# MLP 1 of a four-block transformer step: six of eight fc1 groups as block products, fc2 by groups of four fc1 tiles, job tiles issued by SP

## The chip, the core and the metric

The kernel runs on one core of one Trainium2 chip. The metric is device time in microseconds (us) of one execution. Five engines work side by side, each with its own in-order queue: PE (TensorE, matmuls; PEld is its weight load), DVE (VectorE), ACT (ScalarE), POOL (GpSimd) and SP (SyncE, which here only issues DMAs). They wait for each other on semaphores.

## The reference, cut to what matters

The reference runs 512 latent tokens and 256 context tokens of width 1024 through two blocks of a first model (layers l0, l1) and two of a second (s0, s1). The part touched is the MLP of l0, which handles latents and context together, 768 tokens:

```python
def _sq_relu_mlp(h, w1, w2):          # w1: 1024 x 4096, w2: 4096 x 1024
    a = jnp.maximum(h @ w1, 0)
    return (a * a) @ w2

h = x * (1 + sc2) + sh2
x = _layer_norm(DEEPNORM_ALPHA * x + g2 * _sq_relu_mlp(h, w_fc1[l], w_fc2[l]), ln2_g[l], ln2_b[l])
```

Shift, scale and gate come from a modulation product `silu(c) @ w_mod[l] + b_mod[l]` for two conditions. All values are float32.

## The kernel before, in words

Features lie on the 128 partitions, tokens along the free axis. A matmul of full precision is made of three: each operand is split into a high part (rounded, a copy by ACT) and a low part (the rest, a subtraction by DVE), and PE adds high x high, low weight x high, high weight x low. So each weight tile, 128x1024 (512 KB), is loaded by SP (L537), copied by ACT (`act_split`, L590) and subtracted by DVE (`dve_split`, L622). High parts have NS = 3 buffers: the copy of tile a waits until PE is through tile a - 3. A list written once for all engines (`tile_order`) fixes the order of the tiles; every engine walks it with `pe_tiles`, `act_tiles`, `dve_tiles`.

MLP 1 (l0) is `mlp`: four quarters, each eight fc1 tiles and then eight fc2 tiles. A tile is 8 steps of k with 3 matmuls over 512 and 3 over 256 tokens (L866, L870). fc1 results go to PSUM in turn to two double banks, ACT takes the ReLU (L1252), DVE squares (L1276), ACT makes the high part (L1254), DVE the low part (L1279). fc2 results are added, gated, into the residual by DVE (`dve_add_gated`, L924).

MLP 2 and 4 (l1, s1; 512 tokens) are `eighths`: eight groups of four fc1 tiles. The first group is plain; the other seven form the 4 tiles as a 2x2 block product after Strassen with seven products instead of eight (`product`, L1378, 24 matmuls of 256 columns each). The sums of weight blocks are made by DVE (`dve_block_sum`, L600), the sums of results too (`sum_of`, L1546), the sums of the token operand once (`operand`, L1524; `operand_high`, `operand_low`). fc2 is done per group: eight outputs of four k steps (`outputs`, L1399, L1404), each added to the residual by DVE (`update`, L1592). Results go to four single banks there. MLP 3 (s0) is `quarters`.

Beside MLP 1 and MLP 3 runs `modulation`: beside MLP 1 132 jobs (128 with a 512 KB tile, 4 that spread a condition). A job is one multiply-and-reduce on DVE (L731) over a tile in a ring of NM = 3 buffers. The jobs are spread over steps 2 to 61 of the MLP's 64 tiles; ACT issues the load of job n + 3 after job n (`act_send`, L691). Weight tiles have NR = 4 landing buffers; XR = 4 more come from the end of l1's attention on.

## Time and profile before

| | us |
|---|---|
| median of 3 runs (lowest, highest) | 2992.75 (2991.43, 2995.24) |
| profiled execution | 2994.86 |
| its span on the core | 2993.5 |
| PE busy | 2843.4 (95%) |
| DVE busy | 1878.0 (63%) |
| ACT busy | 1197.9 (40%) |
| granted TensorE clock, mean | 0.98 |

The profiled execution lies 2.1 us above the median and within the spread of the runs; 1.4 us of it lie outside the span. MLP 1 takes the span from about 515 to 1066 us. Rows of a timeline are start, length, engine, line, operation; several instructions can be merged in one (xN), and a bracket at the end gives the idle time before and what ended it.

### The profile page before, as it was taken

The numbers are of one execution on the slowest core, as the hardware profiler recorded it, in microseconds if no ns is written. First come the engines' busy times: TensorE is split into PE (matmuls) and PEld (weight loads), VectorE is DVE, ScalarE is ACT, GpSimd is POOL, SyncE is SP. The second block draws the span as 40 slices with busy tenths as digits, with TensorE's granted clock in tenths as the row PEclk, the third lists the DMA queues.
The fourth block names the chain that finished last, engine by engine and source line by source line (L and its number), as shares of the span: only waits on it lengthen the run. The fifth ranks groups of instructions, "written<-read, shape, count | busy, mean of one in ns | idle before, by whom it ended". The sixth has DMA issues, their size and how long they took to land. (4 is left out here: it accounts for less than half of the span.)

```text
span 2993.5 us, 43305 instructions
## 1 busy us (share of the span) xinstructions
PE 2843.4 (95%) x17474; PEld 2304.2 (77%) x17474; DVE 1878.0 (63%) x2790; ACT 1197.9 (40%) x1963; POOL 340.7 (11%) x371
## 2 busy tenths in 40 slices
PE   7999999999999989999899999999899999899998
PEld 6766667888888867766688886776567999678896
DVE  3655544656565746664687766546736788567775
ACT  4245543412122242554444545212533444444443
POOL 2022220300000030321301002000420000110000
PEclk9999999999999999999999999999999999999999
DMA  7222001466565511001232332222014555422331
GB/s 282 78 93 85 8 16 49 163 196 210 171 211 189 190 56 51 13 15 57 90 99 78 106 120 64 95 64 64 8 59 159 164 182 168 143 62 87 106 106 64
DMA packets 88495, 315.98 MB, mean 106 GB/s; under 512 B 9991, under 2 KB 12295, under 8 KB 88040
## 3 DMA queue, kind: packets, MB, share of 16 engines
q1 hardware_dynamic: 59040, 213.94, 22.3%
q10 hardware_dynamic: 29256, 99.26, 10.0%
q8 instruction: 140, 2.29, 0.3%
q14 instruction: 59, 0.48, 0.0%
HBM read 311.06 MB, written 2.10 MB: 105 GB/s over the span
## 5 line engine op out<-in xcount | busy, mean ns | idle before, releaser
L866 PE MATMUL bank<-t 128*128 128x512 f32 x4064 | 1011.1, 360 | 24.7 <-DVE t L622 7.7
L866 PEld LDWEIGHTS bank<-t 128*128 128x128 f32 x4064 | 673.1, 190 | 163.1 <-issue 40.5
L590 ACT ACTIVATE t<-t 128x1024 fp32r<-128x1024 f32 x410 | 431.0, 1055 | 759.4 <-PE bank L870 253.9
L622 DVE TENSOR_TENSOR t<-t 128x1024 fp32r<-128x1024 f32 x410 | 508.5, 1244 | 328.3 <-ACT t L590 324.1
L870 PE MATMUL bank<-t 128*128 128x512 f32 x2032 | 606.7, 358 | 4.4 <-POOL t L1181 4.2
L870 PEld LDWEIGHTS bank<-t 128*128 128x128 f32 x2032 | 335.1, 190 | 71.0 <-POOL t L1181 10.3
L1399 PE MATMUL bank<-t 128*128 128x512 f32 x1024 | 308.8, 397 | 1.6 <-ACT t L1469 1.6
L1378 PEld LDWEIGHTS bank<-t 128*128 128x128 f32 x2352 | 283.0, 189 | 4.1 <-ACT t L590 2.3
L1378 PE MATMUL bank<-t 128*128 128x256 f32 x2352 | 283.8, 282 | 2.1 <-ACT t L590 2.1
L1399 PEld LDWEIGHTS bank<-t 128*128 128x128 f32 x1024 | 190.0, 188 | 56.0 <-issue 4.8
L731 DVE SCALAR_TENSOR_TENSOR t<-t 128x1024 f32<-128x1024 f32 x176 | 209.3, 1223 | 2.2 <-DMA t<-in_mod 1.8
L1404 PE MATMUL bank<-t 128*128 128x512 f32 x512 | 187.2, 396 | 0.0
L1898 POOL TENSOR_SCALAR t<-t 128x768 f32<-128x768 f32 (+3 forms) x160 | 125.7, 789 | 522.8 <-DVE t L1866 522.7
L924 DVE SCALAR_TENSOR_TENSOR t<-bank,t 128x512 f32<-128x512 f32 (+1 forms) x128 | 81.6, 664 | 148.5 <-PE bank L870 131.3
L1697 PE MATMUL bank<-t 64*128 64x384 f32 (+2 forms) x768 | 137.0, 475 | 16.5 <-ACT t L1796 5.2
L1841 DVE TENSOR_REDUCE t<-bank 128x1 f32<-128x768 f32 (+1 forms) x120 | 96.6, 846 | 88.3 <-PE bank L1706 68.1
L1786 ACT ACTIVATE t<-bank 128x384 f32<-128x384 f32 (+1 forms) x160 | 73.6, 460 | 172.4 <-PE bank L1714 172.0
L1714 PEld LDWEIGHTS bank<-t 128*128 128x128 f32 x784 | 85.8, 141 | 58.7 <-issue 29.9
L1714 PE MATMUL bank<-t 128*128 128x128 f32 x784 | 121.2, 283 | 10.0 <-DVE t L1852 7.0
L1796 ACT ACTIVATE t<-bank,t 128x768 f32<-128x768 f32 (+3 forms) x160 | 124.1, 780 | 14.1 <-DVE t L1841 8.0
L992 ACT ACTIVATE t<-t 128x512 f32<-128x512 f32 (+1 forms) x64 | 43.8, 684 | 214.7 <-DVE t L924 126.4
L1592 DVE SCALAR_TENSOR_TENSOR t<-bank,t 128x512 f32<-128x512 f32 x128 | 93.7, 747 | 48.1 <-PE bank L1404 47.8
(363 smaller groups left out, 3387.9 us busy)
## 6 DMA issues: line engine op xcount, KB each, us to landing
t<-in_mod ACTq DMA_DIRECT2D x176, 512.0 KB, 4.4
t<-in_l0fc SPq DMA_DIRECT2D x64, 512.0 KB, 4.2
t<-in_l1fc SPq DMA_DIRECT2D x64, 512.0 KB, 3.6
t<-in_s0fc SPq DMA_DIRECT2D x64, 512.0 KB, 3.7
t<-in_s1fc SPq DMA_DIRECT2D x64, 512.0 KB, 3.6
t<-in_mod SPq DMA_DIRECT2D x48, 512.0 KB, 4.4
t<-in_mixin SPq DMA_DIRECT2D x24, 512.0 KB, 3.6
t<-in_l0in SPq DMA_DIRECT2D x12, 512.0 KB, 3.8
```

The costliest lines, as they stand in the source:

```text
L590: act.activation(high_of(key), landed_of(key), ACT.Copy).then_inc(*up("act_whi", a))
L622: dve.tensor_tensor(low_of(key), landed_of(key), high_of(key).bitcast(F32), ALU.subtract).then_inc(*up("dve_wlo", a))
L731: dve.scalar_tensor_tensor(x, x, 1.0, sil[:, :], ALU.mult, ALU.mult, accum_out=modt[L][:, j, s:s + 1]).then_inc(*up("dve_job", (name, n)))
L866: pe.matmul(acc.ap[:, o:o + m], w[:, ws], Hh[:, k, o:o + m], start=k == order[0] and w is hi, stop=False)
L870: ins = pe.matmul(acc.ap[:, o:o + m], hi[:, ws], Hl[:, k, o:o + m], start=False, stop=k == order[-1])
L1378: ins = pe.matmul(dst, w[:, ws], x, start=pair == 0 and k == 0 and w is hi and x is high, stop=pair == 1 and k == 3 and x is low)
L1399: pe.matmul(banks[s].ap, w[:, ws], Ah[:, k, :], start=first and w is hi, stop=False)
L1404: ins = pe.matmul(banks[s].ap, hi[:, ws], Al[:, k, :], start=False, stop=last)
L1697: ins = pe.matmul(places[side][:, 512 * r + o:512 * r + o + m], g["q"][side](c), g["k"][side][:, k0:k0 + m], start=r not in begun, stop=last)
L1714: ins = pe.transpose(turns[r].ap[:, P * b:P * b + P], p[:, P * i:P * i + P], mat("ident"))
L1796: act.activation(keys_of(p, g), scores_of(ps[side], g), ACT.Exp, bias=row[:, 7:8], accum_out=row[:, 3:4]).then_inc(*ps[side].freed((tag, u ...
L1898: pool.tensor_scalar(x, x, stat(u, side)[:, 7:8], 1.0, ALU.mult, ALU.mult).then_inc(*up("pool_prob", (tag, u, side)))
```

## The change

MLP 1 is now `eighths` too, for 768 tokens: groups 0 and 1 plain, groups 2 to 7 as block products of 384 columns (`PLAIN_GROUPS`, `G` in the functions). A product needs two matmul targets of 384 columns, that is a double bank, and of these there are three (`ps0`, `ps1`, `ps2`), against four single ones for 512 tokens. fc2 outputs alternate between two of them. The jobs are spread over steps 2 to 123: a plain group has 24 steps (3 at each fc1 tile, 3 at each fc2 tile), a product group 13 (3, 3, 3, 4 at its four fc2 tiles). Their loads are issued by SP, sorted among the weight tiles by place. The extra four landing buffers come from the end of l0's attention on. `mlp` is gone; names in `quarters` change only.

```diff
@@ memory and order
-                self.slot[key], self.slot_after[key] = NR + a - G, ("l1out", 1)
+                self.slot[key], self.slot_after[key] = NR + a - G, ("l0out", 1)
+PLAIN_GROUPS = {"l0": 2, "l1": 1, "s0": 2, "s1": 1}
@@ mlp_order, for l0, l1, s1
+    for Q in range(8):
+        if Q < PLAIN_GROUPS[name]:
+            for m in range(0 if Q else 2, 4):
+                t.tile((name + "fc1", 4 * Q + m))
+        else:
             t.quad(name + "fc1", Q)
         for j in range(4):
             t.tile((name + "fc2", 4 * Q + j))
@@ sp_tiles
-        for _, _, i, send in sorted(tiles + mods, key=lambda x: x[0:2]):
+        jobs = [(place, place, n, send) for place, n, send in sent_jobs]
+        for _, _, i, send in sorted(tiles + mods + jobs, key=lambda x: x[0:2]):
             send(i)
@@ modulation
-        def act_send(n):
+        def sp_send(n):
             L, condition, s, j = jobs[tiles_[n]]
-            act.dma_start(modw[:, n % NM, :], din[f"mod{L}"][j]).then_inc(*up(f"job_in{n % NM}", (name, n), 16))
+            SPQ.wait_ge(*(at("dve_job", (name, n - NM)) if n >= NM else at("pe_mod", seq.mods[seq.mod_keys[-1]])))
+            sp.dma_start(modw[:, n % NM, :], din[f"mod{L}"][j]).then_inc(*up(f"job_in{n % NM}", (name, n), 16))
@@ eighths
+                *steps, pool_all = modulation(name, sil, jobs, 2, 124, lambda step: eighths_place(name, G, step))
+    PRODUCT_BANKS = {NT: (0, 1, 2, 3, 0, 2, 3), T: (2, 0, 1, 2, 1, 2, 0)}
+    OUT_BANKS = {NT: (1, 0, 2, 3), T: (1, 0)}
+        places = {key: fours[m % 4] if n == NT else ps[m % 4 % 3] for m, key in enumerate(first)}
+    def steps_behind(G, Q, j):
+        if Q < G:
+            return range(24 * Q + 12 + 3 * j, 24 * Q + 15 + 3 * j)
+        o = 24 * G + 13 * (Q - G)
+        return range(o + 3 * j, o + 3 * j + (4 if j == 3 else 3))
+    def eighths_place(name, G, step):
+        for Q in range(8):
+            for j in range(4):
+                if step in steps_behind(G, Q, j):
+                    return seq.place[fc2(name, Q, j)] - 0.5
+                if Q < G and step in steps_beside(G, Q, j):
+                    return seq.place[fc1(name, 4 * Q + j)] + 0.2
@@ act_eighths and dve_eighths, a plain group
                 for m in range(4):
-                    dve_tiles(fc1(name, 0, min(m + 2, 3)))
-                    evict(m)
+                    dve_tiles(fc1(name, 4 * Q + min(m + 2, 3)))
+                    evict(Q, m)
+                    if step:
+                        for s in steps_beside(G, Q, m):
+                            step(s)
@@ dve_eighths, each fc2 tile
-                dve_tiles(fc2_pair(name, Q, j))
+                dve_tiles(fc2(name, Q, j))
...
+                if step:
+                    for s in steps_behind(G, Q, j):
+                        step(s)
                 for m in (2 * j, 2 * j + 1):
                     update(Q, m)
```

**Place 1: DVE at fc2.** On DVE, before, two neighbouring fc2 tiles of MLP 1's first quarter (L622 weight split, L731 job, L924 update of the residual from PSUM, double bank 1 and then 0):

```order
L622 TENSOR_TENSOR t5<-t4,t3 128x1024 [waits s_act_whi,s_tile_in2]
L731 SCALAR_TENSOR_TENSOR t2,t17<-t2,t63 128x1024 [waits s_job_in0]
L731 SCALAR_TENSOR_TENSOR t2,t17<-t2,t63 128x1024 [waits s_job_in1]
L924 SCALAR_TENSOR_TENSOR t1<-bank1,t16,t1 128x512 [waits s_pe_tile,s_pool_x]
L924 SCALAR_TENSOR_TENSOR t1<-bank1,t16,t1 128x256
L622 TENSOR_TENSOR t5<-t4,t3 128x1024 [waits s_act_whi,s_tile_in3]
```

Now, on DVE, the first fc2 tile of group 0 (L612 split, L714 job, L1548 update):

```order
L612 TENSOR_TENSOR t5<-t4,t3 128x1024 [waits s_act_whi,s_tile_in2]
L714 SCALAR_TENSOR_TENSOR t2,t17<-t2,t63 128x1024 [waits s_job_in0]
L714 SCALAR_TENSOR_TENSOR t2,t17<-t2,t63 128x1024 [waits s_job_in1]
L714 SCALAR_TENSOR_TENSOR t2,t17<-t2,t63 128x1024 [waits s_job_in2]
L714 SCALAR_TENSOR_TENSOR t2,t17<-t2,t63 128x1024 [waits s_job_in0]
L1548 SCALAR_TENSOR_TENSOR t1<-bank1,t16,t1 128x512 [waits s_pe_half,s_pool_x]
L1548 SCALAR_TENSOR_TENSOR t1<-bank1,t16,t1 128x256
L1548 SCALAR_TENSOR_TENSOR t1<-bank0,t16,t1 128x512 [waits s_pe_tile,s_pool_x]
L1548 SCALAR_TENSOR_TENSOR t1<-bank0,t16,t1 128x256
```

A tile has two outputs instead of one, and its jobs stand between the split and both of the updates.

**Place 2: ACT at the start of a plain group.** On ACT, before, a tile inside MLP 1's first quarter (L590 split of a weight tile, L1252 ReLU out of a bank, L1254 high part, L691 loads for jobs):

```order
L590 ACTIVATE t3<-t4 128x1024 [waits s_tile_in1]
L1252 ACTIVATE t56<-bank0 128x768 [waits s_pe_tile]
L1254 ACTIVATE t53<-t58 128x768 [waits s_dve_asq]
L691 DMA t2<-in_mod1 128x1024 [waits s_dve_job] x2
L590 ACTIVATE t3<-t4 128x1024 [waits s_tile_in2]
```

Now, on ACT, the start of group 1 (L580 split, L1414 ReLU, L1419 high part):

```order
L580 ACTIVATE t3<-t4 128x1024 [waits s_pe_tile,s_tile_in2]
L580 ACTIVATE t3<-t4 128x1024 [waits s_pe_tile,s_tile_in3]
L580 ACTIVATE t3<-t4 128x1024 [waits s_pe_tile,s_tile_in0]
L1414 ACTIVATE t62<-bank0 128x768 [waits s_dve_alo]
L1419 ACTIVATE t60<-t62 128x768 [waits s_dve_asq]
L580 ACTIVATE t3<-t4 128x1024 [waits s_pe_tile,s_tile_in1]
L1414 ACTIVATE t62<-bank1 128x768 [waits s_dve_alo]
```

Three weight splits stand ahead of the group's first ReLU; the third of them waits for PE to be through the group's second fc1 tile.

**Place 3: DVE from the last product to the first outputs.** On DVE, now, group 2 (L1502 sum of a product out of its bank, L1529 low part, L590 sum of weight blocks); before, MLP 1 has no such place:

```order
L1502 TENSOR_TENSOR t62<-bank0,t62 128x768 [waits s_pe_tile]
L1529 TENSOR_TENSOR t61<-t62,t60 128x2x384 [waits s_act_a,s_act_ahi] x2
L612 TENSOR_TENSOR t52<-t51,t3 128x1024 [waits s_act_whi,s_tile_in7]
L590 TENSOR_TENSOR t4<-t51 128x1024 [waits s_tile_in6,s_tile_in5]
L714 SCALAR_TENSOR_TENSOR t2,t17<-t2,t63 128x1024 [waits s_job_in0,s_b7_read,s_b6_read]
L714 SCALAR_TENSOR_TENSOR t2,t17<-t2,t63 128x1024 [waits s_job_in1]
L714 SCALAR_TENSOR_TENSOR t2,t17<-t2,t63 128x1024 [waits s_job_in2]
L1548 SCALAR_TENSOR_TENSOR t1<-bank1,t16,t1 128x512 [waits s_pe_half]
L1548 SCALAR_TENSOR_TENSOR t1<-bank1,t16,t1 128x256
```

The last product and the second output share bank 0; between the bank's reading and the first update stand two low parts, a split, a block sum and three jobs. At the first fc2 tile of the six product groups stand 3, 3, 4, 4, 3, 3 jobs, and at the last 4, 4, 4, 5, 5, 3.

## Rows read from the trace of the kernel before

**Rows 1.** page, part 1: busy us (share of the span) and instructions of each engine

```profile
PE 2843.4 (95%) x17474; PEld 2304.2 (77%) x17474; DVE 1878.0 (63%) x2790; ACT 1197.9 (40%) x1963; POOL 340.7 (11%) x371
```

**Rows 2.** stretches of MLP 1: length, busy PE, PEld, DVE, ACT, POOL; PEclk, DMA share, GB/s

```profile
536.00:603.00 67.00, 67.00 (x386) 58.55 (x387) 46.51 (x57) 23.45 (x27) 15.03 (x8) 1.00 0.61 202
...
938.00:1005.00 67.00, 67.00 (x385) 58.45 (x384) 45.61 (x60) 19.99 (x22) 0.00 (x0) 1.00 0.61 194
```

**Rows 3.** timeline (start, length, engine, line, operation), PE in MLP 1: two k steps that follow each other

```profile
650.67 0.51 PE L870 MATMUL bank<-t 128*128 128x512 f32 x2
...
651.72 0.51 PE L870 MATMUL bank<-t 128*128 128x512 f32 x2
```

**Rows 4.** timeline, PE in MLP 4 (s1): a group's products, then its fc2

```profile
2722.67 20.16 PE L1378 MATMUL bank<-t 128*128 128x256 f32 x168
2742.72 2.09 PE L1399 MATMUL bank<-t 128*128 128x512 f32 x8
...
2748.42 0.63 PE L1399 MATMUL bank<-t 128*128 128x512 f32 x2
...
2755.43 0.62 PE L1399 MATMUL bank<-t 128*128 128x512 f32 x2
```

**Rows 5.** groups by line and shape, 600 to 1300 us: count | busy us, mean ns | idle before

```profile
L731 DVE SCALAR_TENSOR_TENSOR t<-t 128x1024 f32<-128x1024 f32 x114 | 134.7, 1221 | 1.4 <-DMA t<-in_mod 1.1
...
L622 DVE TENSOR_TENSOR t<-t 128x1024 fp32r<-128x1024 f32 x70 | 86.8, 1242 | 73.1 <-ACT t L590 72.0
...
L924 DVE SCALAR_TENSOR_TENSOR t<-bank,t 128x512 f32<-128x512 f32 x32 | 24.0, 751 | 74.7 <-PE bank L870 72.9 <-ACT t L721 1.6
L1279 DVE TENSOR_TENSOR t<-t 128x768 fp32r<-128x768 f32 x24 | 23.0, 959 | 21.9 <-ACT t L1254 21.9
...
L1254 ACT ACTIVATE t<-t 128x768 fp32r<-128x768 f32 x24 | 20.3, 846 | 26.9 <-DVE t L1276 26.9
...
L924 DVE SCALAR_TENSOR_TENSOR t<-bank,t 128x256 f32<-128x256 f32 x32 | 15.2, 475 | 0.0
```

**Rows 6.** timeline, POOL and DVE at the start of MLP 1

```profile
535.82 5.36 POOL L1185 TENSOR_SCALAR t<-t 128x768 f32<-128x768 f32 x3
...
537.39 1.19 DVE L1276 TENSOR_TENSOR t<-t 128x768 f32<-128x768 f32 x1 [0.47 <-ACT t L1252]
```

**Rows 7.** timeline, start of MLP 2 (l1): operand sums, fc2, third ReLU, PE's wait

```profile
1465.72 5.69 DVE L1524 TENSOR_TENSOR t<-t 128x1024 f32<-128x1024 f32 x4
...
1478.38 2.29 PE L1399 MATMUL bank<-t 128*128 128x512 f32 x8
...
1481.23 0.58 ACT L1464 ACTIVATE t<-bank 128x512 f32<-128x512 f32 x1
...
1483.37 0.96 PE L1399 MATMUL bank<-t 128*128 128x512 f32 x3 [1.25 <-ACT t L1469]
```

**Rows 8.** timeline, MLP 4: from the seventh product's sum to the update

```profile
2743.24 0.68 DVE L1546 TENSOR_TENSOR t<-bank,t 128x512 f32<-128x512 f32 x1
...
2743.96 0.63 ACT L1481 ACTIVATE t<-t 128x512 f32<-128x512 f32 x1 [0.86 <-DVE t L1546]
...
2745.88 0.69 DVE L1573 TENSOR_TENSOR t<-t 128x512 fp32r<-128x512 f32 x1 [1.36 <-ACT t L1484]
2746.83 1.23 DVE L622 TENSOR_TENSOR t<-t 128x1024 fp32r<-128x1024 f32 x1 [0.26 <-ACT t L590]
...
2749.11 1.41 DVE L1592 SCALAR_TENSOR_TENSOR t<-bank,t 128x512 f32<-128x512 f32 x2
```

**Rows 9.** page, part 6: DMA issues, us to landing

```profile
t<-in_mod ACTq DMA_DIRECT2D x176, 512.0 KB, 4.4
```

**Rows 10.** timeline, DVE in MLP 1: two jobs in a row

```profile
640.98 1.22 DVE L731 SCALAR_TENSOR_TENSOR t<-t 128x1024 f32<-128x1024 f32 x1
...
642.12 1.22 DVE L731 SCALAR_TENSOR_TENSOR t<-t 128x1024 f32<-128x1024 f32 x1
```

**Rows 11.** view by stretches, norm and start of MLP 1; columns as in rows 2

```profile
518.00:522.00 4.00, 3.77 (x14) 2.83 (x13) 4.00 (x8) 4.00 (x8) 2.71 (x3) 0.57 0.03 6
```

More of the change, by code:

```diff
@@ L299, in eighths_order @@
             t.tile((name + "fc2", 4 * Q + j))
-    t.mark((name, "end"))
-def mlp_order(t, name):
-    t.tile((name + "fc1", 0))
-    t.tile((name + "fc1", 1), 1)
-    for q in range(4):
-        for m in range(NK):
-            if 8 * q + m > 1:
-                t.tile((name + "fc1", 8 * q + m))
-            t.mark((name, "evict", q, m))
-        for m in range(NK):
-            t.tile((name + "fc2", 8 * q + m))
     t.mark((name, "end"))
@@ L374, in first_order @@
     t.mark((name, "ln1"))
[L375 removed]
+    mlp_order(t, name)
 def tile_order():
@@ L679, in jobs_of, with modulation @@
         return [(L, condition, s, None)] + [(L, condition, s, j) for j in range(16 if s else 48)]
-    def modulation(name, sil, jobs, first, last):
+    sent_jobs = []
+    def modulation(name, sil, jobs, first, last, place):
         tiles_ = [i for i, job in enumerate(jobs) if job[3] is not None]
@@ L750, in pool_all @@
                         ins.then_inc(*(up("pool_mod", L) if part == 4 else up("pool_own")))
+        for n in range(NM):
+            sent_jobs.append((seq.place[name + "fc1", 0] - 0.5, n, sp_send))
+        for step in range(first, last):
+            for n in (number[i] + NM for i in due(step) if i in number):
+                if n < len(tiles_):
+                    sent_jobs.append((place(step), n, sp_send))
         return pe_step, act_step, dve_step, pool_all
@@ L1305, in eighths @@
-    def eighths(L, name, N, after, centered, make_h, columns, beside=None, weights=None):
-        n, half = NT, 256
+        half = n // 2
         keys = [out_of(name, 7, m) for m in range(NK)]
@@ L1398, in high @@
                 for w in (hi, lo):
-                    pe.matmul(banks[s].ap, w[:, ws], Ah[:, k, :], start=first and w is hi, stop=False)
+                    for o, m, _ in ranges:
+                        pe.matmul(banks[s].ap[:, o:o + m], w[:, ws], Ah[:, k, o:o + m], start=first and w is hi, stop=False)
             def low(s, k, last):
@@ L1403, in low @@
                 ws = slice(512 * s + P * k, 512 * s + P * k + P)
-                ins = pe.matmul(banks[s].ap, hi[:, ws], Al[:, k, :], start=False, stop=last)
+                for o, m, _ in ranges:
+                    ins = pe.matmul(banks[s].ap[:, o:o + m], hi[:, ws], Al[:, k, o:o + m], start=False, stop=last)
                 if last:
@@ L1443, in pe_eighths, with act_eighths @@
                     beside(4 * Q + j)
+                if step:
+                    for s in steps_behind(G, Q, j):
+                        step(s)
         pe_norm_step(M, 7, acc_of[keys[0]].after(keys[0]))
-        for bank in fours:
-            PEQ.wait_ge(*bank.after(bank.order[-1]))
+        if n == NT:
+            for bank in fours:
+                PEQ.wait_ge(*bank.after(bank.order[-1]))
         pe_tiles((name, "end"))
-    def act_eighths(name, htag, Hh, Tr, T3, Th, Ah, cells, M, beside):
-        half = NT // 2
+    def act_eighths(name, G, htag, n, Hh, Tr, T3, Th, Ah, cells, M, beside, step):
+        half = n // 2
         def operand_high(t):
@@ L2772, in second_h, with quarters_place, place @@
                                ALU.subtract).then_inc(*up("pool_hlo", (N.tag, k)))
-    PRODUCT_BANKS = (0, 1, 2, 3, 0, 2, 3)
-    CELLS = (0, 3, 1, 2)
-    OPERANDS = {1: 0, 2: 1, 4: 2, 5: 3}
+    QUARTER_BANKS = (0, 1, 2, 3, 0, 2, 3)
+    QUARTER_OPERANDS = {1: 0, 2: 1, 4: 2, 5: 3}
+    def quarters_place(name):
+        def place(step):
+            if step < 8:
+                return seq.place[name + "fc1", step] + 0.2
+            q, m = (0, step - 8) if step < 16 else divmod(step // 2, 8)
+            return seq.place[name + "fc2", 8 * q + m] - 0.5
+        return place
     def quarters(L, N, after, columns, jobs):
         name = f"s{L - 2}"
-        keys = [fc2(name, 3, m) for m in range(NK)]
+        keys = [fc2_quarter(name, 3, m) for m in range(NK)]
         with ExitStack() as S:
@@ L2877, in pe_quads @@
             PEQ.wait_ge(*bank.claim((name, "quads")))
-        first = [fc1(name, 0, m) for m in range(NK)]
+        first = [fc1(name, m) for m in range(NK)]
         pe_dense(first[0:2], Hh, Hl, hh, hl, LAT, dict(zip(first, fours)))
```

478 lines of the change are left out of this document (201 added, 277 removed).

## The prediction, made before the changed kernel was run

> **What bounds the kernel now.** Read the page's first part first: PE is busy for 95% of the span, DVE for 63% [rows 1]. Then the view by stretches for MLP 1: PE has no idle time in it, the clock is full, and DVE is busy for 46 of 67 us, ACT for 23 [rows 2]. So MLP 1 is bound by PE, and a change there is worth what it takes from PE, less the time in which PE comes to wait. DVE has about a third of its time free, but a job, a weight split and a residual update must each be done where they stand in its queue; whether they are in time is a matter of order, not of share. The timeline then gives the steps from which I lay the new order out by hand.
>
> **What the change takes from PE.** A k step of 6 matmuls takes 1.05 us [rows 3], a tile 8.4, the four fc1 tiles of a group 33.6. A product has 24 matmuls of 384 columns, which no row shows. A 256-column one takes 119 ns (168 in 20.05 us), a 512-column one 234 ns (30 in 7.01 us) [rows 4]; these are the ends: seven products between 20.0 and 39.3 us, for six groups a gain of 81 or a loss of 34. I take 175 ns, half of the 350 that a 512 and a 256 together take [rows 3], which is 384 columns on average: 4.2 us a product, 29.4 a group. Gain 4.2 x 6 = **25.2 us**. fc2 stays at 33.6 a group.
>
> The Trainium skill ("TensorE: Matmul & The Clock Gate", Part 1: The HAM clock gate) puts a matmul at full clock at columns / 2.4 GHz + 2.5 ns from start to start, 162.5 ns for 384. The trace is slower at both known widths (109 and 216 by the page, against 119 and 234), so its rows decide; by the page for the new matmuls alone the gain would be 38, which is a mixture of two measures.
>
> **What it costs.** DVE pieces, from start to start: job 1.14 [rows 10]; weight split plus block sum 2.28 together [rows 8]; a 768-wide square or low part 0.95; an update 0.75 + 0.475, 1.15 with their overlap; ACT's 768-wide piece 0.85 [rows 5]. A job tile takes 4.4 us from issue [rows 9]; with three buffers a fourth job in a row starts not before 1.2 + 4.4 = 5.6 us after the first, instead of 3.4.
>
> *Group 0.* It begins as the trace has it: fc1 0 and 1 done at 536.6, DVE free at 536.9 [rows 6]. Now the four operand sums come first: 5.69 us at 1024 elements with POOL beside them [rows 7], 8.5 at 1536: DVE is free at 545.4, the split of fc1 3 is ready at 546.8, 1 us after PE wants it; fc1 3 ends at 555.3. Meanwhile DVE does a split, square, low part, three jobs, square, low part, three jobs (evictions of tiles 0 to 2; the high part by ACT lies between square and low part, 0.9). ACT's ReLU of tile 3 stands behind the high part of tile 2 and comes at 561.7. MLP 2, without jobs, shows the same seam: fc1 ends at 1478.4, the fourth ReLU comes 2.85 us later and PE waits 1.25 us [rows 7]; two runs of three jobs (6.9) make up most of the difference. The first output's partner uses the same double bank 0, and PE claims both at once: PE idle 555.3 to 562.6, 7.3 us. Its eight k steps end at 571.4. DVE has still to do: square and low part of tile 3 (until 568.9), three jobs, a split, four jobs (the tiles of these seven come late by the 5.6 us rule: 581.4), update: 582.5. The third output needs that bank: PE idle 11.2 us. From there DVE and PE run abreast (waits of 0.4 and 1.3, with the 1 us at the start) and PE enters group 1 at 609.1 instead of 587.9: **21.2 us**.
>
> *Group 1.* On ACT three splits stand ahead of the first ReLU (place 2), the third waits for fc1 5, done at 625.9; DVE, with the same three ahead of it, idles for some 12 us. Then four evictions with 4, 3, 3, 3 jobs; the load of fc2 5 stands in SP's queue behind four jobs' loads and holds a split until 644.4. ReLU of tile 7 done at 653.4 against fc1 7 done at 642.7: PE idle 10.7 us. Low part, three jobs, split, block sum, four late jobs: first update done at 673.6, PE ready at 662.4 (0.5 of it a wait for the high part): 11.2 us. The low parts of the operands (4 x 1.85, 1.5 times a split) at the next three fc2 tiles cost 3.3 and 1.4: **27.3 us**.
>
> *Groups 2 to 7.* From the last product's end, as 0: DVE's sum from 0.3 to 1.25 (in MLP 4 it starts at 0.5, DVE being busy until then [rows 4, 8]); the second output shares its bank, so PE idles 1.2. Then, as in rows 8 with 768 for 512: three ACT pieces (2.5), low part at 3.85, split 4.8, block sum 5.95, three jobs 7.1 to 10.5, update to 11.7. PE is through the first two outputs at 1.25 + 8.4 = 9.65 and waits 2.1 us. So 3.3 us a group; with four jobs at this place (groups 4 and 5) the fourth comes late, another 3.4; five jobs at the last tile (5 and 6) 1.1 more each. Sum 6 x 3.3 + 6.8 + 2.2 = **28.8 us**. Later outputs are covered: DVE needs 2.3 + 3.4 + 2.3 = 8.0 for a pair, PE 8.4. In the products DVE has 15 of 29 us to do.
>
> Bounds of the waits: the one for the shared bank cannot be covered, so at least 1.2 x 6 = 7 us in all; upwards, each tile that comes late can cost its 4.4 us again.
>
> *The clock.* After the sparse norm stage PE works at half clock (0.57 in 518 to 522) [rows 11], about 6 us from its first matmul, so 3 us lost. Two or three idles of 7 to 12 us may do the same; most of the loss falls in the next wait. I take **3 us**. The Trainium skill ("TensorE: Matmul & The Clock Gate", Part 1: The HAM clock gate) lets the clock follow how busy PE has been, 1.2 GHz after idling and 2.4 after work; a stall of several us is then paid twice, which is part of rival C.
>
> *At nothing:* the loads issued by SP instead of ACT (ACT is busy for 23 of 67 us before [rows 2]; the same engines carry them); four landing buffers from MLP 1 on; MLP 3's jobs (bound: 2 us either way by loads that stand behind others); MLP 2 and 4, whose order is unchanged.
>
> Sum: -25.2 + 21.2 + 27.3 + 28.8 + 3 = **+55 us** on the profiled execution's 2994.9, so 3050; that one lies 2.1 above the median of the runs: **3048 us**.
>
> **Rivals.**
> *A. The waits are half as long.* Loads of jobs come in less than 4.4 us while little else runs, DVE catches up inside a group. For it: DVE waited for a job tile only once in MLP 1, 1.1 us [rows 5]. Against it: there no more than three jobs stood in a row, here seven with one split between. The four longest idles (7.3, 11, 11, 11) rest mostly on order. 77 / 2 - 25 = +13 to +30: 3006 to 3023, say 3015.
> *B. Faster.* PE is the bound and DVE's free third takes up the new work; only the shared bank is seen, 7.4 us, and a few us in group 0. For it: PE never waited in MLP 1 [rows 2], and MLP 4 runs its products without a gap [rows 4]. Against it: MLP 4 has no jobs and a fourth bank, both of which make the difference. -25 + 12 = -13: 2980. It holds if the jobs before the first update are done before PE's first two outputs, that is if DVE gets from the seventh product to the update in 9.65 us rather than 11.7.
> *C. Loads run dry.* Weight tiles that stand in SP's queue behind job loads come late too (one 4.4 us in each of groups 2 to 7, 26 us), or the half clock bites fully (3 us at each of six idles above 5 us): 3075 to 3090.
>
> **How the numbers follow.** Forecast 60%, A 18%, B 10%, C 12%. The forecast's own range is 3032 to 3066, a quarter of its 77 us of waits either way. For 8 in 10 I leave B and the upper half of C out: 3004 to 3076. About 0.2% (6 us) is what a measurement of this kernel can tell from no change. Faster: B, 9%; within: 3%, from the edges of A and B; slower: 88%.
>
> **What the new profile would show.** Product matmuls (L1318) 175 ns apart; if not, the gain is wrong. In the view by stretches PE idle in MLP 1 some 75 us, two thirds of it in the first 160 us. PE's waits put down to DVE L1548 (updates), to ACT L1414 in groups 0 and 1, and to L1502 at each product group's end. DVE idle before L714 on DMA. MLP 1 ending near 1120 instead of 1066. The prediction is wrong in kind if PE's idle time there is below 25 us; if it is there but elsewhere, the step of that group is wrong.

## The result, and the profile after

The changed kernel takes 3078.23 us (median of four runs, 3073.39 to 3081.73) against 2993.04 for the kernel before on the same chip: a ratio of 1.0279, 95% interval 1.0267 to 1.0291, slower by 85 us. Forecast was 3048 (+55), range 3004 to 3076. The direction was right, and so were the engines and lines that PE waits for; the size was not. The profiled execution took 3073.39 us, its span is 3072.1, 78.6 more than before. It is the fastest of the four, so its difference is 6.6 us smaller than that of the medians; the sums below are made on spans.

In the changed kernel the matmuls of fc1 are L855 and L859, a product is L1318, fc2's outputs are L1340 (high parts) and L1346 (low part), the update is L1548, a job L714, a weight split L612 (DVE) behind L580 (ACT), the ReLU of a plain group L1414, a sum of products L1502. First the page's part 1, which answers to [rows 1]:

```profile
PE 2845.3 (93%) x17330; PEld 2319.7 (76%) x17330; DVE 1989.2 (65%) x2922; ACT 1241.0 (40%) x2015; POOL 345.7 (11%) x371
```

PE is as busy as before (2 us more) although it has 144 matmuls less to do; so part of its work became slower. The stretches of MLP 1, one for groups 0 and 1 and their seam and one for each product group (columns as in [rows 2]), show where:

```profile
536.00:603.00 67.00, 50.82 (x266) 43.59 (x265) 55.23 (x71) 14.12 (x17) 19.14 (x8) 0.87 0.58 202
603.00:670.00 67.00, 50.67 (x274) 43.41 (x272) 37.16 (x53) 16.53 (x17) 0.00 (x0) 0.90 0.49 167
670.00:706.00 36.00, 29.59 (x155) 25.55 (x156) 34.43 (x49) 4.52 (x4) 0.00 (x0) 0.86 0.52 182
706.00:772.00 66.00, 63.11 (x357) 58.21 (x356) 48.76 (x64) 21.57 (x26) 0.00 (x0) 1.00 0.49 158
772.00:841.00 69.00, 65.24 (x372) 60.29 (x371) 51.84 (x69) 22.60 (x26) 0.98 (x5) 1.00 0.50 162
841.00:917.00 76.00, 67.98 (x370) 62.41 (x369) 51.38 (x69) 22.59 (x26) 0.00 (x0) 0.96 0.45 145
917.00:988.00 71.00, 65.48 (x363) 60.31 (x362) 52.87 (x71) 21.63 (x24) 0.00 (x0) 0.98 0.51 166
988.00:1055.00 67.00, 63.80 (x360) 58.62 (x359) 52.43 (x70) 21.62 (x24) 0.00 (x0) 1.00 0.51 170
1055.00:1141.00 86.00, 73.86 (x411) 63.51 (x414) 52.40 (x69) 27.17 (x31) 0.00 (x0) 0.96 0.42 145
```

PE stood still for 74.5 of these 605 us (530.5 busy), where [rows 2] have none, and the clock, full before, is below 1.00 in six of the nine stretches. The norm matmuls behind MLP 1's last output start at 1140.0 instead of 1065.7, so 74.3 of the 78.6 us lie in MLP 1 (timeline, PE, first the kernel before):

```profile
1065.71 0.62 PE L968 MATMUL bank<-t 128*32 128x512 f32 x2
...
1139.99 0.62 PE L957 MATMUL bank<-t 128*32 128x512 f32 x2
```

The waits behind the idle time are, in the view of waits for PE, 536 to 1141 us (waiting line, releaser: us in total, times, longest):

```profile
PE bank L1340 <- DVE t L1548: 44.9, 13, 8.9
PE bank L1340 <- ACT t L1414: 19.0, 2, 11.1
PE bank L1340 <- DVE t L1502: 7.5, 6, 1.3
PE bank L1318 <- DVE t L1548: 1.5, 2, 1.2
```

The first three are the waits that the prediction named, and the third is the shared bank: six times 1.25 us, where it gave 1.2. The seams of groups 0 and 1 answer to [rows 7]; timeline, PE:

```profile
562.08 5.46 PE L1340 MATMUL bank<-t 128*128 128x512 f32 x16 [7.88 <-ACT t L1414]
581.65 1.62 PE L1340 MATMUL bank<-t 128*128 128x512 f32 x4 [8.12 <-DVE t L1548]
```

fc2 of group 0 starts at 562.1 (laid out by hand: 562.6), its third output at 581.7 (582.5); group 1 starts at 610.1 (609.1), its fc2 at 655.1 (653.4), the third output at 675.0 (673.6), group 2 at 705.5 (703.6). So the first 170 us took as long as forecast, though not for the same reasons: PE is idle for 38.9 us of them, not for 48.5, and 20.8 us of its work run at half clock. What was missed in the total lies in the product groups. They take 66.9, 68.6, 76.0, 70.9, 67.4 and, to the last output's end, 84.7 us. That is 50.1 more than six times 63.0 (the forecast's 29.4 and 33.6), 4.3 for the last one's norm matmuls and 2.1 for the transposes of two conditions, the last two of which the kernel before pays too; the forecast had 28.8.

One place shows three of the missed pieces at once. Group 4, timeline of PE:

```profile
885.06 1.15 PE L1340 MATMUL bank<-t 128*128 128x512 f32 x4 [4.25 <-DVE t L1548]
...
895.09 1.04 PE L693 MATMUL bank<-t 128*128 128x128 f32 x8
898.64 1.08 PE L1340 MATMUL bank<-t 128*128 128x512 f32 x4 [2.51 <-DVE t L1548]
```

ACT in the same stretch, the copy of the condition:

```profile
896.16 1.08 ACT L704 ACTIVATE t<-bank 128x512 f32<-128x512 f32 x2 [14.20 <-PE bank L693]
```

And DVE, the updates of the third and fourth output:

```profile
897.35 2.19 DVE L1548 SCALAR_TENSOR_TENSOR t<-bank,t 128x512 f32<-128x512 f32 x4 [6.83 <-ACT t L704]
```

The transposes of a condition (L693) stand on PE behind fc2's third and fourth output; ACT copies their result, and DVE has this step in its queue ahead of the updates of these same outputs. So DVE idles for 6.8 us with an output ready, and PE, which needs that bank, comes out 3.5 us later (1.0 transposing, 2.5 idle). Group 3 has the same ahead of its third output. And around both waits of group 4 the clock falls; view by stretches, the clock is the third number from the end:

```profile
885.00:889.00 4.00, 3.94 (x14) 3.33 (x15) 4.00 (x5) 0.00 (x0) 0.00 (x0) 0.58 0.68 241
889.50:893.00 3.50, 3.50 (x23) 3.06 (x22) 1.02 (x2) 0.00 (x0) 0.00 (x0) 1.00 0.75 232
899.00:902.00 3.00, 3.00 (x12) 2.56 (x11) 2.90 (x5) 0.00 (x0) 0.00 (x0) 0.55 0.02 5
903.00:906.00 3.00, 3.00 (x19) 2.65 (x18) 3.00 (x7) 0.00 (x0) 0.00 (x0) 1.00 0.56 161
```

After 4.25 us of idle time PE works at the lower of its two levels (1.2 GHz) and then at the full one again; after 2.51 us it did so here, but not in group 3. The Trainium skill ("TensorE: Matmul & The Clock Gate", Part 1: The HAM clock gate) has the clock follow how busy PE has been; the rows agree, with a mean granted clock of 0.58 behind the wait of 4.25 us.

In the last group the norm's steps stand among the updates, and a term for them was lacking too. The first two of these waits lie in MLP 1, the third behind it (1.1 us in the kernel before); timeline, PE:

```profile
1106.86 1.15 PE L1340 MATMUL bank<-t 128*128 128x512 f32 x4 [3.94 <-DVE t L1548]
...
1128.32 1.62 PE L1340 MATMUL bank<-t 128*128 128x512 f32 x4 [4.47 <-DVE t L1548]
...
1148.29 1.07 PE L957 MATMUL bank<-t 128*32 128x512 f32 x2 [6.80 <-ACT t L981]
```

### The profile page after: what moved, and what is told of

It reads as the page before. It is cut to its first block and busy times, and to the rows that moved or that the text cites. A ratio compares the mean times of both kernels' runs of the same rounds, so it can differ in the third digit from the quotient of the medians.

```text
span 3072.1 us, 43261 instructions
## 1 busy us (share of the span) xinstructions
PE 2845.3 (93%) x17330; PEld 2319.7 (76%) x17330; DVE 1989.2 (65%) x2922; ACT 1241.0 (40%) x2015; POOL 345.7 (11%) x371
## 5 line engine op out<-in xcount | busy, mean ns | idle before, releaser
L580 ACT ACTIVATE t<-t 128x1024 fp32r<-128x1024 f32 x428 | 449.5, 1054 | 779.1 <-PE bank L1346 377.2
L612 DVE TENSOR_TENSOR t<-t 128x1024 fp32r<-128x1024 f32 x428 | 529.9, 1242 | 320.4 <-ACT t L580 316.5
L855 PE MATMUL bank<-t 128*128 128x512 f32 x2272 | 624.4, 378 | 22.2 <-ACT t L1161 7.7
L1340 PE MATMUL bank<-t 128*128 128x512 f32 (+1 forms) x2048 | 537.5, 376 | 73.8 <-DVE t L1548 44.9
L855 PEld LDWEIGHTS bank<-t 128*128 128x128 f32 x2272 | 399.4, 192 | 120.1 <-issue 38.5
L1340 PEld LDWEIGHTS bank<-t 128*128 128x128 f32 x2048 | 356.4, 194 | 159.9 <-issue 69.7
L1318 PE MATMUL bank<-t 128*128 128x256 f32 (+1 forms) x3360 | 462.2, 298 | 2.7 <-DVE t L1548 1.5
L1318 PEld LDWEIGHTS bank<-t 128*128 128x128 f32 x3360 | 459.6, 188 | 5.6 <-issue 2.9
L859 PE MATMUL bank<-t 128*128 128x512 f32 x1136 | 377.1, 376 | 5.2 <-POOL t L1170 4.9
L1346 PE MATMUL bank<-t 128*128 128x512 f32 (+1 forms) x1024 | 314.5, 371 | 0.0
L859 PEld LDWEIGHTS bank<-t 128*128 128x128 f32 x1136 | 198.1, 191 | 51.7 <-POOL t L1170 11.3
L714 DVE SCALAR_TENSOR_TENSOR t<-t 128x1024 f32<-128x1024 f32 x176 | 208.4, 1219 | 15.7 <-DMA t<-in_mod 15.4
L1548 DVE SCALAR_TENSOR_TENSOR t<-bank,t 128x512 f32<-128x512 f32 (+1 forms) x256 | 165.1, 678 | 73.0 <-PE bank L1346 63.7
L1346 PEld LDWEIGHTS bank<-t 128*128 128x128 f32 x1024 | 176.9, 192 | 36.6 <-DVE t L1529 2.6
L1502 DVE TENSOR_TENSOR t<-bank,t 128x512 f32<-128x512 f32 (+1 forms) x140 | 107.7, 769 | 58.7 <-PE bank L1318 55.5
L590 DVE TENSOR_TENSOR t<-t 128x1024 f32<-128x1024 f32 x104 | 130.8, 1258 | 0.0
L1677 PEld LDWEIGHTS bank<-t 128*128 128x128 f32 x784 | 86.0, 141 | 58.7 <-issue 30.0
```

The source lines that it names most:

```text
L580: act.activation(high_of(key), landed_of(key), ACT.Copy).then_inc(*up("act_whi", a))
L590: dve.tensor_tensor(landed_of(k[p]), landed_of(k[a]), landed_of(k[b]), op).then_inc(*up("dve_sum", k[p]))
L612: dve.tensor_tensor(low_of(key), landed_of(key), high_of(key).bitcast(F32), ALU.subtract).then_inc(*up("dve_wlo", a))
L714: dve.scalar_tensor_tensor(x, x, 1.0, sil[:, :], ALU.mult, ALU.mult, accum_out=modt[L][:, j, s:s + 1]).then_inc(*up("dve_job", (name, n)))
L855: pe.matmul(acc.ap[:, o:o + m], w[:, ws], Hh[:, k, o:o + m], start=k == order[0] and w is hi, stop=False)
L859: ins = pe.matmul(acc.ap[:, o:o + m], hi[:, ws], Hl[:, k, o:o + m], start=False, stop=k == order[-1])
```

## The experiments

Each run has its own measurement of the kernel before beside it, whose medians lay between 2994.3 and 2996.7 us; so kernels are compared by their ratios to it, and 0.001 is 3 us. The changed kernel's ratio is 1.0279 throughout. Each ratio has its 95% interval in brackets; half of one is 2.5 to 5 us.

**Jobs of 8 elements.**

```diff
-dve.scalar_tensor_tensor(x, x, 1.0, sil[:, :], ALU.mult, ALU.mult,
+dve.scalar_tensor_tensor(x[:, 0:8], x[:, 0:8], 1.0, sil[:, 0:8], ALU.mult, ALU.mult,
```

> The changed kernel with MLP 1's 128 jobs cut to 8 of their 1024 elements; their loads, waits and places stay. It leaves most of the modulation products out, so that its output is not the reference's. Theory O (DVE's own time for the jobs, standing in its queue ahead of evictions and updates, makes the waits): of some 74 us of PE idle time in MLP 1 about 20 stay (1.25 x 6 for the shared bank, about 3 for the fourth ReLU in each of groups 0 and 1, condition steps and the last group's norm steps), the half clock goes with the long waits; 2993 - 25 + 20 + 3 to 8 = 2990 to 3000 us. Theory L (the tiles of the jobs land too late, whatever DVE does): the waits stay, above 3040 us. Theory K (MLP 1 is slow by the products and the half clock themselves): above 3040 as well, but with little idle time.

Measured: 3043.47 us, 1.0158 (1.0141 to 1.0175). 36 us go, not the 80 of theory O. The time lies within the "above 3040" of theories L and K; with 51 us of idle time left it is not K, and L holds in part only, since its waits do not all stay. PE's idle time in MLP 1 still has most of the same places; view of waits, 536 to 1117 us, PE:

```profile
PE bank L1340 <- DVE t L1548: 30.3, 11, 7.7
PE bank L1340 <- ACT t L1414: 10.8, 2, 6.0
```

And of DVE, whose jobs now wait for their loads:

```profile
DVE t L714 <- DMA t<-in_mod: 51.9, 29, 3.6
```

A job that costs DVE under 0.2 us instead of 1.14 still waits for its 512 KB tile. The changed kernel has 15.4 us of such waits, so DVE's time for the jobs hid the other 36 of these 52.

**The same, and no loads after the first three.**

```diff
-DVEQ.wait_ge(*at(f"job_in{n % NM}", (name, n)))
+DVEQ.wait_ge(*at(f"job_in{n % NM}", (name, n % NM)))
+if n >= NM:
+    DVEQ.wait_ge(*at("dve_job", (name, n - NM)))
@@ modulation
-                if n < len(tiles_):
-                    sent_jobs.append((place(step), n, sp_send))
+                pass
```

> As the run with jobs of 8 elements (3043 us), and without the loads of the job tiles after the first three; it leaves most of the modulation products out, so that its output is not the reference's. That run still had 53 us of PE idle time in MLP 1, and DVE stood before a job for its load 29 times, 52 us in all. Theory L (loads that land late, in DVE's queue ahead of evictions and updates, make what was left): the 7.7 and 6.3 us before the third outputs of groups 0 and 1 and about half of the 4.7 and 6.0 before the first ones go, and the weight tiles behind the loads come earlier: 3043 - 13 - 5 - 5 (half clock) = 3020, between 3008 and 3028. Theory W (the order alone: ReLU behind splits, shared bank, condition steps, norm steps): the waits stay, 3035 to 3043.

Measured: 3011.46 us, 1.0058 (1.0043 to 1.0073), within theory L's range: another 30 us. So DVE's time for the jobs and their loads together make 66 of the 85 us. What is left above the kernel before, 17 us, is the new form with next to no work in the jobs (the four conditions are still spread): 4.8 us before fc2 of group 0 (ReLU), 1.25 us six times, 2.5 at two conditions, 3.9 + 1.3 in the last group and 3.6 behind it are the larger gaps of its timeline. It means that in this order the products would not have paid even without the jobs' work and loads.

**Updates ahead of the jobs.**

```diff
-                if step:
-                    for s in steps_behind(G, Q, j):
-                        step(s)
                 for m in (2 * j, 2 * j + 1):
                     update(Q, m)
+                if step:
+                    for s in steps_behind(G, Q, j):
+                        step(s)
```

> The changed kernel with both residual updates of an fc2 tile ahead of that tile's jobs on DVE instead of behind them. Theory O: the third output's wait in each product group (2.1 us, 5.5 with four jobs) goes, 12.6 + 6.8 = 19, and of the 8 to 9 us before the third output in groups 0 and 1 about 4 each go, and with the waits above 4 us some half clock; 3078 - 27 = 3051, between 3040 and 3060. Theory D (DVE is simply behind in these stretches, so the same jobs delay the next pair of outputs): the wait moves to the fifth output and little is won, 3070 to 3078.

Measured: 3045.66 us, 1.0167 (1.0151 to 1.0182), 34 us less than the changed kernel, theory O. The waits put to L1548 fall from 44.9 to 21.9 us. New ones come: the split of a weight tile now waits for its load 8 times, up to 15.0 us, and PE for the split twice before products (view of waits, 536 to 1115 us, ACT and PE):

```profile
ACT t L580 <- DMA t<-in_l0fc: 59.8, 8, 15.0
```

```profile
PE bank L1318 <- ACT t L580: 3.9, 2, 2.1
```

In the changed kernel only one weight tile is later than 2.5 us, the 12.4 us of group 1.

**A third bank for fc2's outputs.**

```diff
-    OUT_BANKS = {NT: (1, 0, 2, 3), T: (1, 0)}
+    OUT_BANKS = {NT: (1, 0, 2, 3), T: (1, 2, 0, 1, 2, 1, 0, 1)}
@@ outputs
+            of = (1, 0) if n == T and Q == 7 else OUT_BANKS[n]
```

> The changed kernel with fc2's outputs in groups 0 to 6 of MLP 1 going round three double banks instead of two (1, 2, 0, 1, 2, 1, 0, 1). Theory O: the 1.25 us for the shared bank goes in five or six groups (7), and the wait for the first update is at the fourth output instead of the third, 4.2 us later, so a wait of 2.1 disappears and one of 5.5 falls to 1.3: 3 to 4 x 2.1 + 2 x 4.2 + 2 x 4.2 in groups 0 and 1, about 24 with the shared bank 31: 3047, between 3038 and 3058. Theory D: DVE is behind for a whole group and the waits only move, 3068 to 3078.

Measured: 3049.71 us, 1.0182 (1.0165 to 1.0198), 29 us less, as theory O has it. Only the last group, which keeps two banks, still shows the 1.25 us (view of waits, PE, L1503 being the sum):

```profile
PE bank L1341 <- DVE t L1549: 25.1, 11, 5.0
PE bank L1341 <- ACT t L1420: 11.9, 3, 5.3
PE bank L1341 <- ACT t L1415: 7.9, 2, 6.9
PE bank L1318 <- DVE t L1549: 5.2, 4, 2.5
PE bank L1341 <- DVE t L1503: 1.3, 1, 1.3
```

**No products.**

```diff
-PLAIN_GROUPS = {"l0": 2, "l1": 1, "s0": 2, "s1": 1}
+PLAIN_GROUPS = {"l0": 8, "l1": 1, "s0": 2, "s1": 1}
-                *steps, pool_all = modulation(name, sil, jobs, 2, 124,
+                *steps, pool_all = modulation(name, sil, jobs, 2, 190,
```

> The changed kernel with no products in MLP 1: all eight groups as plain fc1 tiles, fc2 by four fc1 tiles, jobs 15 or 16 a group, no operands. Theory O: each group after the first costs as group 1 does without its operands (about 20 us: the ReLU behind three splits, the jobs ahead of the first update), 8 x 67.2 + 15 + 7 x 20 = 693 us for MLP 1 instead of 615: about 3155 us. Theory S (the waits are a matter of the first 160 us, later groups run level): MLP 1 at 538 + 40 to 60, 3035 to 3055 us.

Measured: 3124.03 us, 1.0423 (1.0406 to 1.0441), 43 us above the changed kernel, nearer to theory O. The later plain groups wait 9 to 13 us each, not 20, at the same three places. So it is fc2 by groups of four with its queues, not the products, that loses the time; the products win some of it back.

**The three edits of order together.** Updates first, third bank, and:

```diff
-                    act_tiles(fc1(name, 4 * Q + min(m + 2, 3)))
+                    act_tiles(fc1(name, 4 * Q + (m if Q else min(m + 2, 3))))
```

(the same on DVE).

> The changed kernel with three edits of order: updates ahead of jobs, outputs round three banks, and in group 1 one weight split ahead of each eviction instead of three ahead of the first. If each removes what the traces of the single runs put to it: from 3046 (updates first) less 7.5 for the shared bank, 8 of group 1's 12.9 us before its first output, 6 before the third and fifth outputs of groups 0 and 1, 4 in the product groups and 4 of half clock: 3016, between 3006 and 3028. If the waits have one cause in common (DVE behind by its whole load), 3038 to 3046.

Measured: 3009.43 us, 1.0049 (1.0032 to 1.0066). 69 us go, within the forecast of 3006 to 3028. All jobs are done and all tiles loaded, and yet it takes as long as the run with tiny jobs and no loads. Most of the 66 us were thus the price of where the jobs stand. It does not follow that the jobs cost nothing in this order: the three edits also take away waits that the run without loads still has, five of the six of 1.25 us and the two of 2.51 at conditions, 11 us in all. How fast the new order is without jobs was not run.

**Jobs spread over the products too.** In the product groups seven of 13 steps stand with the seven products:

```diff
+                    if step:
+                        step(step_with(G, Q, p))
@@ steps_behind
-        o = 24 * G + 13 * (Q - G)
-        return range(o + 3 * j, o + 3 * j + (4 if j == 3 else 3))
+        o = 24 * G + 13 * (Q - G) + 7
+        return range(o + (0, 2, 4, 5)[j], o + (2, 4, 5, 6)[j])
```

> The three edits of order, and of each product group's 13 steps of jobs seven stand with the seven products and six at fc2 (2, 2, 1, 1) instead of 13 at fc2. DVE has 15 of 29 us to do in the products, so seven jobs (8 us) fit there, their loads have a product's 4.2 us each, and DVE reaches fc2 with at most two jobs to a tile. If late jobs still cost in groups 2 to 7: 5 to 10 us less than the three edits alone, about 3008. If instead the jobs delay the sums that free the products' banks: the same or up to 10 us more than the three edits alone, with PE waiting before products.

Measured: 2998.92 us, 1.0019 (1.0010 to 1.0028), 9 us less than without. PE is idle for 21 us of MLP 1; the view by stretches:

```profile
536.00:1074.00 538.00, 516.58 (x2920) 467.08 (x2918) 437.79 (x594) 174.60 (x195) 22.74 (x18) 0.98 0.54 186
```

Between 705 and 1023 us there is no gap of 0.8 us or more: five product groups without a longer wait. There the products bring their gain in full.

**Extra matmuls in the waits.**

```diff
+            fill = {0: (26 if Q < 2 else 0, 0), 1: (26 if Q < 2 else 6 if Q < 7 else 12, 0), ...}
+                for _ in range(fill[s]):
+                    pe.matmul(b6.ap[:, :], Hh[:, 0, 0:P], Hh[:, 0, 0:512], start=True, stop=True)
```

> The changed kernel with extra matmuls (512 columns, into a bank nobody reads) in places where PE would wait: 26 ahead of the first and the third output of groups 0 and 1 (6 us each of waits of 8 to 11), 6 ahead of the third output of groups 2 to 6, 12 ahead of the third and the eighth of group 7. Theory C (an idle of some us makes the half clock that follows, and PE works its next 7 to 14 us at half speed): nearly no half clock in groups 2 to 7, where it cost (9.8 + 6.5) / 2 = 8 us, and in groups 0 and 1, where the next wait hides most of it, 2 to 4: 3078 - 11 = 3067, between 3063 and 3072. Theory N (the clock has nothing to do with these waits, or costs nothing): 3076 or more, since the extra matmuls can only take time.

Measured: 3073.72 us, 1.0268 (1.0253 to 1.0283): 3 us less by the ratios, inside both intervals, and between the numbers of the two theories. PE's idle time fell to 47 us, but 2.7 us were still left at the third output of group 4, and the clock fell all the same (view by stretches):

```profile
886.00:889.00 3.00, 3.00 (x11) 2.52 (x11) 3.00 (x5) 0.00 (x0) 0.00 (x0) 0.52 0.78 251
```

So this run decides nothing on the price of the half clock; the fillers were too few to keep it up. Theory C's "next 7 to 14 us" counts idle time as well: behind each of the four long waits of groups 0 and 1 the changed kernel has 3.6 to 6.1 us of work at the lower level.

**Loads by ACT again.** In the changed kernel, `act_send` as before the change.

```diff
-            SPQ.wait_ge(*(at("dve_job", (name, n - NM)) if n >= NM else ...))
-            sp.dma_start(modw[:, n % NM, :], din[f"mod{L}"][j])...
+            act.dma_start(modw[:, n % NM, :], din[f"mod{L}"][j])...
@@ act_step
+                if i in number:
+                    n = number[i]
+                    if n + NM < len(tiles_):
+                        ACTQ.wait_ge(*at("dve_job", (name, n)))
+                        act_send(n + NM)
```

> The changed kernel with one part undone: MLP 1's and MLP 3's job tiles issued by ACT, each behind the job that frees its buffer, as before the change. Theory B (three buffers and 4.5 us a load against four to seven jobs in a row, whoever issues): DVE still waits for job tiles, 15 us or so, and the time is 3072 to 3084 us. Theory Q (loads that stand behind weight tiles in SP's queue, and weight tiles behind them): the 12.4 us wait for fc2 5's tile goes, DVE's waits for job tiles fall below 5 us, and the time is 3045 to 3065 us.

Measured: 3084.13 us, 1.0293 (1.0277 to 1.0309), at the upper edge of theory B and 20 us above theory Q. The 12.4 us for fc2 5's tile are gone, without use; DVE still waits 17.0 us for job tiles (view of waits, where a job is L722):

```profile
DVE t L722 <- DMA t<-in_mod: 17.0, 13, 2.9
```

and ACT, which now waits for jobs, is late with the ReLU of group 0 (14.6 us of PE idle time instead of 7.9). So the late job tiles do not come from SP's queue. That they come from three buffers and 4.5 us a load is the theory left, worked out but not shown: no run had a fourth buffer.

**The kernel before, loads by SP.** The reverse edit in the kernel before.

```diff
-            act.dma_start(modw[:, n % NM, :], din[f"mod{L}"][j])...
+            SPQ.wait_ge(*(at("dve_job", (name, n - NM)) if n >= NM else ...))
+            sp.dma_start(modw[:, n % NM, :], din[f"mod{L}"][j])...
```

> The kernel before with one edit: the tiles of the jobs of MLP 1 and MLP 3 issued by SP among the weight tiles instead of by ACT, as the change does. My prediction put this at nothing (2 us either way). Rival: the loads that stand in SP's queue behind a wait for a job's buffer hold weight tiles back, as in the changed kernel, where a split waited 12.4 us for its tile: 3005 or more, with PE idle time in MLP 1, where it has none.

Measured: 2991.6 us, 0.9982 (0.9973 to 0.9992). MLP 1 has no idle time here either. Some 3 us of the gain lie in MLP 3, whose loads the change moves too: from its first plain tile to its last fc2 tiles it takes 299 us instead of 302, and these two waits of PE in the kernel before are gone (2249 to 2552 us):

```profile
PE bank L866 <- ACT t L2922: 1.7, 1, 1.7
PE bank L866 <- DVE t L622: 1.2, 1, 1.2
```

**Conditions ahead of the outputs.**

```diff
                 if step:
                     for s in steps_behind(G, Q, j):
                         step(s)
+                outputs(Q, j)
```

(on PE; `outputs` stood ahead of the steps).

> The changed kernel with the transposes of the condition (four times 8 in MLP 1) on PE ahead of the fc2 outputs beside which the jobs stand, instead of behind them. In the trace of the change the updates of groups 3 and 4 wait for them, 3.5 us each, with 3.4 us of half clock in group 4. If that is a term of its own: 3078 - 7 - 2 = 3069, between 3064 and 3073. If DVE is late there by its jobs anyway: 3075 to 3079.

Measured: 3072.96 us, 1.0252 (1.0238 to 1.0266), 8 us less by the ratios, give or take 5.5, so the size is uncertain. In its timeline the 2.51 us of group 4 are gone. In group 3 2.97 us stay at the same output, put down to the update: there the jobs ahead of it would have been late anyway, and the output starts only 0.8 us earlier (814.8 against 815.6).

**Three more edits on the spread version.** Jobs in steps 12 to 124, the operands' low parts behind the updates, the shift's matmuls ahead of the third output in the last group:

```diff
-modulation(name, sil, jobs, 2, 124,
+modulation(name, sil, jobs, 12, 124,
@@ pe, outputs
+            early = Q == 7 and j == 1 and n == T
+            if early:
+                pe_norm_step(M, 1, acc_of[keys[0]].after(keys[0]))
```

> The spread version (2999 us) with three more edits: jobs from step 12 instead of 2 (none beside the first three evictions, where DVE still has 8.3 us of operand sums), the low parts of the operands behind the updates of their fc2 tile instead of ahead, and in the last group the shift's matmuls ahead of the third output instead of behind it. In the trace of the spread version these places hold 1.1 + 1.5 + 5.2 us (group 0), 4.2 (group 1) and 3.9 (last group) of PE idle time, and 3.4 us lost to half clock behind each of the first two: 16 + 7 = 23. Less what comes late in their place (an eviction's wait of some 3 us in group 0 as in MLP 2): 2999 - 20 = 2979, between 2974 and 2988. If the jobs that stand closer together later cost as much as they did at the start: 2992 to 2999.

Measured: 2999.36 us, 1.0011 (1.0002 to 1.0019). A miss: 2 us, not 20, and those 2 lie inside both intervals. The gaps of group 0 and the 3.9 us of the last group did go, but the jobs now stand closer, and other waits came, 3.0 us in the last group, 5.1 before an output of group 1 and this one before a product of group 2; timeline, PE:

```profile
678.43 1.94 PE L1324 MATMUL bank<-t 128*128 128x384 f32 x5 [3.85 <-issue]
```

DVE, the last of four jobs in a row and the split behind it:

```profile
675.95 1.23 DVE L714 SCALAR_TENSOR_TENSOR t<-t 128x1024 f32<-128x1024 f32 x1 [1.23 <-DMA t<-in_mod]
677.11 1.22 DVE L612 TENSOR_TENSOR t<-t 128x1024 fp32r<-128x1024 f32 x1
```

The fourth job's tile is late, and the product's matmuls go on as the split ends (677.11 + 1.22); the profile names no releaser.

**One plain group.** As the last, with:

```diff
-PLAIN_GROUPS = {"l0": 2, "l1": 1, "s0": 2, "s1": 1}
+PLAIN_GROUPS = {"l0": 1, "l1": 1, "s0": 2, "s1": 1}
-modulation(name, sil, jobs, 12, 124,
+modulation(name, sil, jobs, 22, 113,
```

> As the late start, with one plain group instead of two, so seven product groups, and the jobs in steps 22 to 113. One more group of products takes 33.6 - 29.9 = 3.7 us from PE. DVE then has 15 (sums) + 18.4 (fc2) + 21 us of jobs to a group of 63: 2975 if nothing comes late, down to 2970; if the operands' low parts (7.4 us at fc2 of group 0) are late for the products, 2980 to 2990.

Measured: 2990.37 us, 0.9983 (0.9974 to 0.9991), the median of the kernel before beside it being 2996.72: 5 us faster than the kernel before. It misses the 2975 expected; the seven groups still hold small waits and the last one 4.0 and 2.2. MLP 1 in the view by stretches:

```profile
536.00:1061.00 525.00, 510.39 (x2895) 464.73 (x2893) 446.43 (x600) 181.44 (x203) 23.09 (x18) 0.99 0.54 190
```

Its last output ends 6.2 us before that of the kernel before, and 3.4 us of wait follow instead of 1.1. But the kernel before with its loads issued by SP, an edit that this version holds too, is as fast (0.9982). So products and new order together add nothing that these runs can tell from zero.

**The same, jobs in steps 16 to 104.**

```diff
-modulation(name, sil, jobs, 22, 113,
+modulation(name, sil, jobs, 16, 104,
```

> The version with one plain group (2990 us beside 2997 for the kernel before on the same chip), with the jobs in steps 16 to 104 instead of 22 to 113, so none in the last group, whose three waits were 4.0, 2.2 and 1.0 us with 3.4 us of half clock. If they were the jobs': less 5 to 7, 2984, a ratio of 0.996 to the kernel before. If 1.5 jobs a step crowd the six groups before (DVE 59 of 63 us): 2990 to 2998.

Measured: 2997.41 us, 1.0011 (1.0001 to 1.0021). The last group's waits fell from 7.3 to 2.3 us, and a wait of 7.3 us came in group 1, before a product whose split stood behind jobs with late tiles. Where the jobs go, the wait goes.

## Why the prediction was wrong

**Right.** PE bound MLP 1 and then waited; the releasers were those named; the seams of groups 0 and 1 (their end at 705.5 against 703.6); the shared bank (1.25 us six times, gone in all groups that got a third bank). The order of the work sets the time, and not DVE's share: with the updates first DVE has the same work and 34 us are gone, with the third bank and group 1's splits 69 of the 85.

**Right by luck.** The idle time in all, 74.5 us against 77, agrees only as a sum. Groups 0 and 1 have 38.9 us against 48.5, groups 2 to 7 35.5 against 28.8. So half of it lies in the first 170 us, and not two thirds. The measured time lies within rival C's 3075 to 3090, but C's first half did not happen: no weight tile came late in groups 2 to 7.

**The step that failed: groups 2 to 7, forecast at 28.8 us, measured at 50.1.** By its terms:

- *Half clock, 7.4 us.* The prediction allowed 3 us in all, at groups 0 and 1. By the trace's records of the granted clock PE was busy at half clock for 37 us of MLP 1: 20.8 before group 2, where by the agreement of the seams the following waits hid nearly all of its cost, and 9.8 in groups 4 and 5 and 6.5 in the last, where little is behind them. A k step of group 4 takes 1.92 us there instead of 1.05, so 0.45 of the 16.3 us is lost:

```profile
886.64 1.48 PE L1340 MATMUL bank<-t 128*128 128x512 f32 x4
...
888.56 1.09 PE L1340 MATMUL bank<-t 128*128 128x512 f32 x4
```

  This is rival C's second half, at waits of 4.5 us and below, which the rival did not consider. The size is worked out from the trace; the run that was to show it by itself did not.
- *Last group, 9.1 us* (3.94 + 0.68 + 4.47). The sum treated it as the other five, though the norm's steps stand in its updates. The runs without job work keep the 3.94 and 1.3 of the rest, so some 5 us are the order's and 4 the jobs'.
- *Conditions, 5 us*: 2.5 us of idle time twice. The prediction had no term for them although it counted 132 jobs, four of them of this kind. Their transposes are no part of the miss, since the kernel before does the same 32 in its MLP 1 (view of the line, duration in ns, first and last start):

```profile
L700 PE MATMUL bank<-t x32: 270/273/274, 536.7 to 859.3; 128*128 128x128 f32 x32
```

  In the run that moves them the wait of group 3 stays, as one before the third output; so 2.5 of the 5 could as well be put to the last term below.
- *Product matmuls, 3.2 us.* The tile view of group 3's products gives 177 ns from start to start (29.6 us for 167), not 175:

```profile
L1318 PE MATMUL bank<-t x168: 332/338/342, 772.4 to 802.0; 128*128 128x384 f32 x168
```

  The interpolation between two known widths was good to 1%. By the 162.5 ns that the prediction worked out from the Trainium skill ("TensorE: Matmul & The Clock Gate", Part 1: The HAM clock gate), an estimate, the products would have gained another 15 us, which the trace does not show.
- *fc2's k steps, 3.6 us.* At full clock the 32 k steps of a group take 34.0 us and not 33.6 (group 2: 66.9 less its products of 30.0 and 2.9 of idle time), and in the last group, cut up by the norm's matmuls, another 1.1.
- *Waits before the third output, 7.6 us too many*: 11.8 us (1.64 twice, 4.25, 4.27) against 12.6 + 6.8. This is the only large term that was too high.

The six come to 20.7 of the 21.3 us. On the spans the forecast missed by 23.6 us: 21.3 here, 4.3 behind MLP 1 and 1.9 in groups 0 and 1, less the 3 us that it held for the clock; that is 0.9 too many.

**At nothing, and not nothing.** The loads by SP gain about 5 us in the kernel before (3 of them seen in MLP 3), outside the 2 us that bounded them. Behind MLP 1 the changed kernel nevertheless loses 4.3 us; the norm's wait of 6.8 us at its end, 1.1 in the kernel before, is the largest single piece, and the prediction had no term for it.

**What stays open.** What the half clock costs by itself; whether a fourth buffer for the job tiles would end their waits; and how the 66 us divide between DVE's time and the loads, since each hides the other: the 36 and 30 us hold for this order of taking them away.

## What to carry to other kernels

When small jobs are laid beside a bound engine, lay out the queue of the engine that does them, from the moment a result is ready to the moment its bank is free, and put nothing between the two that can go elsewhere; here the same jobs and loads cost 66 us in one order, and in another the kernel with them is as fast as the first one without, though that order takes away some other waits too. A hand schedule must hold every kind of step in the queue, the rare ones (four conditions, one last group) above all, and a term for the clock wherever it leaves PE idle for some us (7.4 us in groups 2 to 7 here). A gain of matmuls on the bound engine is worth its full size only when the trace shows no wait in that stage. Measure each part of a change by itself, the ones put at nothing too: here the best version of the whole was no faster than one such part alone.
